# Row transposes at the end of their attention step, their low part one step later, splits and norm-weight products on other steps

## The chip, the cores and the metric

The kernel runs on one core of a Trainium2 chip. The core has five engines: TensorE (PE) for matmuls and transposes, VectorE (DVE), ScalarE (ACT), GpSimd (POOL) and SyncE (SP), which here only starts DMAs. Each takes its own instructions in the order in which they are written, and waits at semaphores that others count up. The metric is the device time of one execution in microseconds, lower is better, as the median of several runs.

## The reference

One decoder block on x of 512 rows (SEQ) and 1024 columns, all in float32:

```python
h = rms_norm(x, g_mix_norm)
z = h @ w_in                      # q, k and v of three branches, gates, zu, zv
# 8 heads of 64, in 2 groups: compressed, selected and window attention
o_attn = g0 * o_cmp + g1 * o_sel + g2 * o_win
o_mix = gelu(zu) * (w_s @ rms_norm(gelu(zv)) + sp_b)
o = concat(rms_norm(o_attn, g_out[:512]), rms_norm(o_mix, g_out[512:]))
x = x + o @ w_out
h = rms_norm(x, g_ffn_norm)
x = x + square(relu(h @ w_ff1)) @ w_ff2
```

With 512 rows the selection takes all eight blocks and the window is as long as the sequence, so the selected and the window branch are both causal attention over the keys seen so far, with their own keys and values.

## The kernel before, in words

Rows are cut into four tiles t of 128. A float32 operand of a large product is kept as two parts, a rounded high part (ACT copies it to fp32r) and a low part (DVE subtracts the high part from the source), and each product is three matmuls, high by high, high by low and low by high (the function three, lines L427 to L429). Weights come by DMA into four raw slots, and are split into high and low part in the same way.

Between the input projection and the feed-forward stage runs the attention loop over 64 steps v, each one (row tile t, head h, branch b): sixteen steps for t = 0, and sixteen for each further tile, with t + 1 key tiles in each. Every engine has its own loop over the steps, written out by hand, in which other work is placed by step number. In step v:

- PE computes the scores of step v + 4 (LEAD = 4, L2018), transposes the weighted probabilities of step v (probs_t, L2057), on odd steps multiplies the probabilities of a pair with the values (values, L2076, LAG = 2), and every fourth step turns a result back (turn_back, L2090).
- ACT copies the transposed probabilities as their high part (pt_high, L1065), and takes the exp of step v + 4 (exp, L1057), which needs DVE's row maximum of it; every fourth step it keeps the values' result (ot_keep).
- DVE takes the row maximum of step v + 4 (row_max, L1505), on even steps the reciprocals of a pair of sums (coefs, L1536), and makes the low part of the transposed probabilities (pt_low, L1528); every eighth step it adds a result to o_sb (combine).
- GpSimd weights the probabilities of a pair (L668, L670) when the reciprocals of the pair are there.

Between these stand the jobs, placed by the table JOBS. Row transposes (rows_t, L1784) turn a tile's rows from o_sb into PSUM as four 128x128 transposes: ("mix", 3, 0) in step 1, ("attn", 0, 0) in 34, ("attn", 1, 0) in 40, ("ffn", 0, 0) in 45, ("ffn", 0, 1) in 50, ("attn", 2, 0) in 55. ACT then makes the high part (ht_hi_evac, L785; for ffn it keeps a raw copy first, raw_keep, L1044; both through job_act), and DVE the low part (ht_lo_evac, L1232). Output projections ("mixo" and "attno", tile, half of the columns) are four chunks c of three matmuls in four steps in a row; chunk 0 is at the end of its step, the others near its start. They follow the row transposes: attno 0 0 in 36 to 39, attno 0 1 in 41 to 44, attno 1 0 in 46 to 49, attno 1 1 in 51 to 54, attno 2 0 in 56 to 59. DVE adds a finished one to xs (add, L1558) at the last of its four steps. All jobs of the loop use one PSUM bank, JB = 3, and each waits until the one before it is taken: a projection until the low part is made, a row transpose until the add is done.

Further work in the loop that the change touches: the split of the feed-forward weights' units 0 and 1 (unit_hi on ACT, L1039; unit_lo on DVE, L1566), 128x1024 each, and ffn_rows (L1226), the product of 512 columns of xs with the norm weight, of which the row transposes of ffn are made: ffn_rows(t, i) must be done before ("ffn", t, i).

After the loop a few more jobs follow in other banks (TAIL). Then comes the feed-forward stage, in units of 24 or 12 matmuls, which is the same before and after.

Of the kernel before, what the change touches and what calls it, by code (L numbers as in the profile page):

```python
# [138 lines left out]
HTN = {k: n for n, k in enumerate(HT)}  # L139
# [78 lines left out]
CHUNKS = {v + c: (k, c) for k, v in JOBS.items() for c in range(steps_of(k))}  # L218
ENDS = {v + steps_of(k) - 1: k for k, v in JOBS.items()}
# [16 lines left out]
def hybrid_block(nc, x, xt, w512, w_c, cmp_w1, cmp_w2, cmp_pe, sp_w, sp_b, g_cols, g_ffn, g_heads, g_sgu,  # L236
                 g_kc, rope, w_ff1, w_ff2, y):
    ctx = ExitStack()
    with ctx:
# [504 lines left out]
        def _(act):  # L744
# [331 lines left out]
            def job_act(k):  # L1076

                if k and k[0] == "ffn":
                    raw_keep(*k[1:])
                if k in HTN:  # L1080
                    ht_hi_evac(*k)
# [6 lines left out]
                exp(v)  # L1088
            for w in range(LEAD, NV + LEAD + LAG):
                s = w - LEAD  # L1090
                job_act(ENDS.get(s))
                if s < NV:
                    pt_high(s)
                if w < NV:
                    exp(w)
                if s >= LAG and (s - LAG) % 4 == 3:
                    ot_keep((s - LAG) // 4)
                if s == 0:
                    ht_hi_evac("mix", 2, 0)
                if s == 2:  # L1100
                    hi(22)
                if s == 10:
                    hi(23)
                if s in (19, 22, 26, 28):
                    hi(24 + (19, 22, 26, 28).index(s))
                if s in (20, 36, 52):
                    act.wait_ge(o_evac, 2 * (s // 16))
                    norm_sum("attn", s // 16 - 1, scr[:, 0:AW])
                if s in (42, 47):
                    unit_hi((s - 42) // 5)  # L1110
                if s in (48, 58):
                    t = (s - 48) // 10
                    act.wait_ge(added, ADD_NO["attno", t, 1] + 1)
                    norm_sum("ffn", t, scr[:, :])
# [71 lines left out]
        def _(dve):  # L1186
# [382 lines left out]
            for w in range(NV + LEAD + LAG + BACK):  # L1569
                s = w - LEAD  # L1570
                k = ENDS.get(s)
                if k in HTN:
                    ht_lo_evac(*k)
                if LEAD <= w < NV:
                    row_max(w)
                if k in ADD_NO:
                    add(*k)
                if 2 <= w <= NV and w % 2 == 0:
                    coefs(w // 2 - 1)
                if 0 <= s < NV:  # L1580
                    pt_low(s)
                if s == 0:
                    ht_lo_evac("mix", 2, 0)
                if s == 3:
                    lo(22)
                if s == 11:
                    lo(23)
                if s in (20, 23, 27, 29):
                    lo(24 + (20, 23, 27, 29).index(s))
                if s in (43, 48):  # L1590
                    unit_lo((s - 43) // 5)
                if s >= LAG + BACK and (s - LAG - BACK) % 8 == 7:
                    combine((s - LAG - BACK) // 16, (s - LAG - BACK) // 8 % 2)
                if s in (41, 45, 52, 56):
                    ffn_rows((s - 41) // 11, {41: 0, 45: 1, 52: 0, 56: 1}[s])


            ffn_rows(2, 0)
# [165 lines left out]
        def _(pe):  # L1764
# [355 lines left out]
            for v in range(NV + LAG):  # L2120
# [5 lines left out]
                product = CHUNKS[v] if v in CHUNKS and CHUNKS[v][0] in ADD_NO else None  # L2126
                if product and product[1] > 0:
                    job(*product)
                if v in CHUNKS and not product:
                    job(*CHUNKS[v])  # L2130
                if v < NV:
                    probs_t(v)
                if v >= LAG:
                    values(v - LAG)
                if product and product[1] == 0:
                    job(*product)
                if v >= LAG + BACK and (v - LAG - BACK) % 4 == 3:
                    turn_back((v - LAG - BACK) // 4)

# [169 lines left out]
```

## Time and profile before

| What | Value |
|---|---|
| median of 3 runs | 591.51 us (590.43 to 591.6) |
| profiled execution | 590.6 us, its span 588.8 us |
| PE busy | 567.9 us, 96% of the span |
| DVE, ACT, POOL busy | 440.7, 359.5, 128.0 us |
| granted TensorE clock | full, in every slice of the span |

The span is what the profile sees of one execution, from the first to the last instruction; the device time lies 1.8 us above it. Busy time of PE is that of its matmuls and transposes, whose modelled ends overlap their successors, so costs are better read from one start to the next. An idle time that the timeline lists stands in brackets behind the instruction that ended it, with what released it.

### The profile page before, as it was taken

The numbers are of one execution on the slowest core, as the hardware profiler recorded it, in microseconds if no ns is written. First come the engines' busy times: TensorE is split into PE (matmuls) and PEld (weight loads), VectorE is DVE, ScalarE is ACT, GpSimd is POOL, SyncE is SP. The second block draws the span as 40 slices with busy tenths as digits, with TensorE's granted clock in tenths as the row PEclk, the third lists the DMA queues.
The fourth block names the chain that finished last, engine by engine and source line by source line (L and its number), as shares of the span: only waits on it lengthen the run. The fifth ranks groups of instructions, "written<-read, shape, count | busy, mean of one in ns | idle before, by whom it ended". The sixth has DMA issues, their size and how long they took to land.

```text
span 588.8 us, 9215 instructions
## 1 busy us (share of the span) xinstructions
PE 567.9 (96%) x3433; PEld 495.8 (84%) x3433; DVE 440.7 (75%) x721; ACT 359.5 (61%) x644; POOL 128.0 (22%) x209
## 2 busy tenths in 40 slices
PE   8999999999889989989999999999999999999997
PEld 7777777887777777868999999999998888888886
DVE  3799890786677878857877675567699996898674
ACT  6866561738676768755673487733697556565551
POOL 1560000002343533510320202211023123020200
PEclk9999999999999999999999999999999999999999
DMA  8933247351112111001997957996879879976862
GB/s 309 336 100 124 93 142 250 107 214 39 53 46 82 37 37 37 1 2 47 188 200 211 176 185 164 187 197 167 208 137 186 216 163 207 243 144 233 175 201 108
DMA packets 25164, 87.56 MB, mean 149 GB/s; under 512 B 3024, under 2 KB 3312, under 8 KB 25120
## 3 DMA queue, kind: packets, MB, share of 16 engines
q0 software_dynamic: 9856, 35.38, 32.1%
q1 hardware_dynamic: 15120, 51.59, 25.3%
q8 instruction: 28, 0.46, 0.3%
q14 instruction: 16, 0.13, 0.1%
q10 hardware_dynamic: 144, 0.00, 0.0%
HBM read 84.87 MB, written 2.10 MB: 148 GB/s over the span
## 4 chain that ended last, share of the span: by engine, by line
PE 80%; DVE 8%; ACT 3%; issue 3%; POOL 3%; DMA 3%; SPq 1%; DVEq 0%; ACTq 0%
PE ps L427 23%; PE ps L429 23%; PE ps L428 23%; PE ps L2057 2%; DMA xT<-in_xt 2%; PE ps L2076 1%; PE ps L1784 1%; PE ps L1927 1%; DMA pe_sb<-in_cmp_pe 1%; DVE ps L1505 1%; DVE w_lo_sb L1203 1%; ACT pt_sb L1065 1%; POOL rope_k L606 1%; PE ps L2018 1%; PE ps L2019 1%
## 5 line engine op out<-in xcount | busy, mean ns | idle before, releaser
L1039 ACT ACTIVATE w_hi_sb<-raw 128x1024 fp32r<-128x1024 f32 x112 | 118.6, 1060 | 114.9 <-PE ps L429 93.3
L1566 DVE TENSOR_TENSOR w_lo_sb<-raw,w_hi_sb 128x1024 fp32r<-128x1024 f32 x112 | 137.1, 1225 | 64.7 <-ACT w_hi_sb L1039 64.4
L680 POOL DMA_DIRECT2D raw<-in_w_ff x64 | 55.5, 867 | 237.5 <-DVE w_lo_sb L1566 213.1
L427 PE MATMUL ps<-w_hi_sb,a_hi 128*128 128x512 f32 x224 | 87.1, 389 | 0.0
L428 PE MATMUL ps<-w_lo_sb,a_hi 128*128 128x512 f32 x224 | 87.1, 389 | 0.0
L429 PE MATMUL ps<-w_hi_sb,a_lo 128*128 128x512 f32 x224 | 87.1, 389 | 0.0
L427 PE MATMUL ps<-w_hi_sb,ht_hi 128*128 128x512 f32 x192 | 78.4, 409 | 4.0 <-DVE ht_lo L1232 1.4
L427 PE MATMUL ps<-ht_hi,w_hi_sb 128*128 128x256 f32 (+1 forms) x272 | 79.1, 291 | 0.0
L429 PE MATMUL ps<-ht_hi,w_lo_sb 128*128 128x256 f32 (+1 forms) x272 | 78.8, 290 | 0.0
L428 PE MATMUL ps<-ht_lo,w_hi_sb 128*128 128x256 f32 (+1 forms) x272 | 78.7, 289 | 0.0
L429 PE MATMUL ps<-w_hi_sb,ht_lo 128*128 128x512 f32 x192 | 75.2, 392 | 0.0
L428 PE MATMUL ps<-w_lo_sb,ht_hi 128*128 128x512 f32 x192 | 75.1, 391 | 0.0
L427 PE MATMUL ps<-S_hi,w_hi_sb 128*128 128x256 f32 x192 | 54.3, 283 | 0.0
L428 PE MATMUL ps<-S_lo,w_hi_sb 128*128 128x256 f32 x192 | 54.3, 283 | 0.0
L429 PE MATMUL ps<-S_hi,w_lo_sb 128*128 128x256 f32 x192 | 54.3, 283 | 0.0
L429 PEld LDWEIGHTS ps<-ht_hi,w_lo_sb 128*128 128x128 f32 x272 | 52.1, 192 | 0.7
L428 PEld LDWEIGHTS ps<-ht_lo,w_hi_sb 128*128 128x128 f32 x272 | 52.2, 192 | 0.6
L427 PEld LDWEIGHTS ps<-ht_hi,w_hi_sb 128*128 128x128 f32 x272 | 52.1, 192 | 0.7
L429 PEld LDWEIGHTS ps<-w_hi_sb,a_lo 128*128 128x128 f32 x224 | 42.0, 188 | 8.8
L427 PEld LDWEIGHTS ps<-w_hi_sb,a_hi 128*128 128x128 f32 x224 | 42.0, 188 | 8.7
L428 PEld LDWEIGHTS ps<-w_lo_sb,a_hi 128*128 128x128 f32 x224 | 42.0, 188 | 8.6
L427 PEld LDWEIGHTS ps<-w_hi_sb,ht_hi 128*128 128x128 f32 x192 | 36.1, 188 | 13.3 <-issue 3.2
(239 smaller groups left out, 1136.3 us busy)
## 6 DMA issues: line engine op xcount, KB each, us to landing
raw<-in_w_ff POOLq DMA_DIRECT2D x64, 512.0 KB, 6.3
raw<-in_w_ff SPq DMA_DIRECT2D x48, 512.0 KB, 4.2
raw<-in_w SPq DMA_DIRECT2D x23, 512.0 KB, 4.4
xs<-in_x SPq DMA_DIRECT2D x8, 512.0 KB, 7.1
raw<-in_cmp_w SPq DMA_DIRECT2D x8, 512.0 KB, 4.3
xT<-in_xt SPq DMA_DIRECT2D x3, 512.0 KB, 9.0
raw<-in_w_c SPq DMA_DIRECT2D x4, 304.0 KB, 3.1
out_y<-xs SPq DMA_DIRECT2D x2, 512.0 KB, 3.2
```

Of the source, the lines that this page charges most:

```text
L427: pe.matmul(out, l_hi, r_hi, start=start, stop=False)
L428: pe.matmul(out, l_hi, r_lo, start=False, stop=False)
L429: return pe.matmul(out, l_lo, r_hi, start=False, stop=stop)
L606: pool.tensor_tensor(out, bc(table, shape), bc(g, shape), ALU.mult).then_inc(rope_made, 1)
L680: pool.dma_start(raw[:, n % RAW, :], (w_ff1, w_ff2)[stage - 1][k, q], accum_op=ALU.add, max_dma_last_dim=8192).then_inc(raw_added[n % RAW] ...
L1039: act.activation(w_hi_sb[:, FS[j], :], raw[:, j, :], ACT.Copy).then_inc(w_hi, 1)
L1065: act.activation(p_parts(v, 0), ps[:, 4 + v % 2, 0:n].rearrange("p (k s) -> p k s", s=P), ACT.Copy).then_inc(pt_hi, 1)
L1203: last = dve.scalar_tensor_tensor(out=l[:, k, :], in0=r[:, k, :], scalar=gcol(n, k), in1=h[:, k, :].bitcast(F32), op0=ALU.mult, op1=ALU.su ...
L1505: dve.tensor_tensor_reduce(out=s, in0=s, in1=causal[:, SEQ - n:], scale=-1.0, scalar=-MASKED, op0=ALU.add, op1=ALU.min, accum_out=nmax[:, ...
L1566: dve.tensor_tensor(w_lo_sb[:, FS[j], :], raw[:, j, :], w_hi_sb[:, FS[j], :].bitcast(F32), ALU.subtract).then_inc(w_lo, 1)
L1784: last = pe.transpose(ps[:, bank, k * P:k * P + P], src[:, k * P:k * P + P], ident[:, :])
L2057: mm = pe.transpose(ps[:, 4 + v % 2, k * P:k * P + P], p_sb[:, v % PB, k * P:k * P + P], ident[:, :])
```

## The change

Four things are moved. On PE the row transposes no longer stand ahead of the step's probability transposes but at its end, behind the values (where chunk 0 of a projection already stands). On ACT the copies of a job (job_act) stand behind pt_high, exp and ot_keep of the step. On DVE the low part (ht_lo_evac) is made one step later, and behind that step's row maximum. The splits of units 0 and 1 are one step earlier on both engines, and the norm-weight products move from steps 41, 45, 52, 56 to 41, 48, 53, 57 (the first argument, the tile, is 0, 0, 1, 1 in both).

```diff
--- before.py
+++ after.py
@@ -1088,13 +1088,13 @@
                 exp(v)
             for w in range(LEAD, NV + LEAD + LAG):
                 s = w - LEAD
-                job_act(ENDS.get(s))
                 if s < NV:
                     pt_high(s)
                 if w < NV:
                     exp(w)
                 if s >= LAG and (s - LAG) % 4 == 3:
                     ot_keep((s - LAG) // 4)
+                job_act(ENDS.get(s))
                 if s == 0:
                     ht_hi_evac("mix", 2, 0)
                 if s == 2:
@@ -1106,8 +1106,8 @@
                 if s in (20, 36, 52):
                     act.wait_ge(o_evac, 2 * (s // 16))
                     norm_sum("attn", s // 16 - 1, scr[:, 0:AW])
-                if s in (42, 47):
-                    unit_hi((s - 42) // 5)
+                if s in (41, 46):
+                    unit_hi((s - 41) // 5)
                 if s in (48, 58):
                     t = (s - 48) // 10
                     act.wait_ge(added, ADD_NO["attno", t, 1] + 1)
@@ -1569,10 +1569,10 @@
             for w in range(NV + LEAD + LAG + BACK):
                 s = w - LEAD
                 k = ENDS.get(s)
-                if k in HTN:
-                    ht_lo_evac(*k)
                 if LEAD <= w < NV:
                     row_max(w)
+                if ENDS.get(s - 1) in HTN:
+                    ht_lo_evac(*ENDS[s - 1])
                 if k in ADD_NO:
                     add(*k)
                 if 2 <= w <= NV and w % 2 == 0:
@@ -1587,12 +1587,12 @@
                     lo(23)
                 if s in (20, 23, 27, 29):
                     lo(24 + (20, 23, 27, 29).index(s))
-                if s in (43, 48):
-                    unit_lo((s - 43) // 5)
+                if s in (42, 47):
+                    unit_lo((s - 42) // 5)
                 if s >= LAG + BACK and (s - LAG - BACK) % 8 == 7:
                     combine((s - LAG - BACK) // 16, (s - LAG - BACK) // 8 % 2)
-                if s in (41, 45, 52, 56):
-                    ffn_rows((s - 41) // 11, {41: 0, 45: 1, 52: 0, 56: 1}[s])
+                if s in (41, 48, 53, 57):
+                    ffn_rows(s // 50, {41: 0, 48: 1, 53: 0, 57: 1}[s])
 
 
             ffn_rows(2, 0)
@@ -2126,14 +2126,12 @@
                 product = CHUNKS[v] if v in CHUNKS and CHUNKS[v][0] in ADD_NO else None
                 if product and product[1] > 0:
                     job(*product)
-                if v in CHUNKS and not product:
-                    job(*CHUNKS[v])
                 if v < NV:
                     probs_t(v)
                 if v >= LAG:
                     values(v - LAG)
-                if product and product[1] == 0:
-                    job(*product)
+                if v in CHUNKS and (not product or product[1] == 0):
+                    job(*CHUNKS[v])
                 if v >= LAG + BACK and (v - LAG - BACK) % 4 == 3:
                     turn_back((v - LAG - BACK) // 4)
```

## Rows read from the trace of the kernel before

**Rows 1.** The page, busy us (share of the span) and instructions of each engine.
```profile
PE 567.9 (96%) x3433; PEld 495.8 (84%) x3433; DVE 440.7 (75%) x721; ACT 359.5 (61%) x644; POOL 128.0 (22%) x209
```

**Rows 2.** Windows: length, busy us of each engine, PE clock, DMA share, GB/s.
```profile
195.00:232.00 37.00, 32.22 (x211) 27.75 (x211) 28.70 (x75) 27.37 (x69) 14.05 (x27) 1.00 0.09 30
...
280.00:580.00 300.00, 300.00 (x1926) 274.76 (x1925) 235.02 (x271) 182.12 (x239) 55.49 (x64) 1.00 0.83 186
```

**Rows 3.** Timeline of PE: start us, us, instructions, idle before them and releaser.
```profile
145.81 0.50 PE L427 MATMUL ps<-w_hi_sb,ht_hi 128*128 128x512 f32 x1 [1.44 <-DVE ht_lo L1232]
...
195.92 0.66 PE L1784 MATMUL ps<-ident,o_sb 128*128 128x128 f32 x4
...
199.60 0.55 PE L2057 MATMUL ps<-ident,p_sb 128*128 128x128 f32 x3 [0.74 <-POOL p_sb L670]
...
206.82 0.60 PE L1784 MATMUL ps<-ident,o_sb 128*128 128x128 f32 x4
207.26 0.49 PE L2057 MATMUL ps<-ident,p_sb 128*128 128x128 f32 x3
207.50 0.42 PE L2018 MATMUL ps<-kT,qT 128*128 128x384 f32 x1
...
208.98 0.40 PE L427 MATMUL ps<-w_hi_sb,ht_hi 128*128 128x512 f32 x1
...
218.01 0.66 PE L1784 MATMUL ps<-ident,o_sb 128*128 128x128 f32 x4 [2.53 <-DVE xs L1558]
218.50 0.49 PE L2057 MATMUL ps<-ident,p_sb 128*128 128x128 f32 x3
...
219.54 0.40 PE L2018 MATMUL ps<-kT,qT 128*128 128x512 f32 x1
...
220.56 0.50 PE L427 MATMUL ps<-w_hi_sb,ht_hi 128*128 128x512 f32 x1
...
229.65 0.65 PE L1784 MATMUL ps<-ident,o_sb 128*128 128x128 f32 x4 [1.33 <-DVE xs L1558]
...
230.50 0.48 PE L2018 MATMUL ps<-kT,qT 128*128 128x512 f32 x1
...
232.44 0.40 PE L427 MATMUL ps<-w_hi_sb,ht_hi 128*128 128x512 f32 x1
...
240.26 0.65 PE L1784 MATMUL ps<-ident,o_sb 128*128 128x128 f32 x4 [0.51 <-DVE xs L1558]
...
242.14 0.38 PE L2090 MATMUL ps<-ident,ot_sb 128*128 128x128 f32 x2
...
243.18 0.48 PE L427 MATMUL ps<-w_hi_sb,ht_hi 128*128 128x512 f32 x1
```

**Rows 4.** Timeline of DVE, steps 34, 40 and 43 to 44.
```profile
197.24 0.69 DVE L1232 TENSOR_TENSOR ht_lo<-ps,ht_hi 128x512 fp32r<-128x512 f32 x1 [0.91 <-ACT ht_hi L785]
...
208.09 0.69 DVE L1232 TENSOR_TENSOR ht_lo<-ps,ht_hi 128x512 fp32r<-128x512 f32 x1 [1.05 <-ACT ht_hi L785]
...
214.21 0.56 DVE L1528 TENSOR_TENSOR pt_sb<-ps,pt_sb 128x384 fp32r<-128x384 f32 x1 [1.06 <-ACT pt_sb L1065]
214.68 1.22 DVE L1566 TENSOR_TENSOR w_lo_sb<-raw,w_hi_sb 128x1024 fp32r<-128x1024 f32 x1
215.81 0.41 DVE L1545 TENSOR_TENSOR o_sb<-o_sb,ps 128x256 f32<-128x256 f32 x1
...
216.60 0.69 DVE L1505 CUSTOM_DVE_ANT_0 ps<-ps,causal 128x512 f32<-128x512 f32 x1
...
217.21 0.75 DVE L1558 SCALAR_TENSOR_TENSOR xs<-ps,rstd,xs 128x512 f32<-128x512 f32 x1
```

**Rows 5.** Timeline of ACT, steps 44 and 45.
```profile
217.38 0.69 ACT L1057 ACTIVATE p_sb<-ps,nmax 128x512 f32<-128x512 f32 x1 [1.85 <-DVE nmax L1505]
...
218.70 0.60 ACT L1044 ACTIVATE ht_raw<-ps 128x512 f32<-128x512 f32 x1 [0.54 <-PE ps L1784]
```

**Rows 6.** Line L1226: count, duration ns min/median/max, first and last start, forms.
```profile
L1226 DVE TENSOR_TENSOR o_sb<-xs,grow_ffn x8: 681/692/1019, 210.9 to 273.4; 128x512 f32<-128x512 f32 x8
```

## Prediction

> **What bounds the kernel.** I read the page's busy shares first: TensorE (PE) is busy 96% of the span, far above the others [rows 1]. Then the windows, since a share over the whole span mixes stages: from 280 to 580 us PE is busy 300.00 of 300.00 us, so the feed-forward stage starts when the attention stage hands over and then runs at its own pace; DVE (235.02) and ACT (182.12) are not full there [rows 2]. The reader is to see that time can only be won or lost ahead of 280 us, and that whatever is won there comes out at the end one for one. Of 195 to 232 us PE is busy only 32.22 of 37.00, so 4.78 us stand open [rows 2]. The timeline of PE then says where: five of its waits hang on the row transposes (L1784). In step 34 they start at 195.92, an estimated 0.27 after PE was through with the scores, which the row does not list as a wait; the probability transposes of step 36 wait 0.74; in step 45 they wait 2.53, in step 50 1.33, in step 55 0.51 [rows 3]. The DVE timeline shows the other face: DVE sits 0.91 and 1.05 us in front of each low part (L1232), because it is first in its step and waits for ACT's high part, and behind it queue the row maximum, the coefficients and the low part of the probabilities [rows 4].
>
> Steps are numbered as in the code. Costs on PE are taken from start to start: row transposes 0.44 (206.82 to 207.26); scores, probabilities and values of a step 1.48 (207.50 to 208.98) and probabilities with values 1.04 (218.50 to 219.54) for three key tiles, so scores 0.44; scores, probabilities and values for four tiles 1.94 (230.50 to 232.44) [rows 3].
>
> **The change, part by part.** No instruction is added or removed: 64 steps with the same matmuls, evictions and loads. Only orders change. So the price is in waits, and I went through each job with its neighbours.
>
> *The new shape of the wait.* Row transposes go into PSUM bank 3, and so does the projection that follows. That projection's chunk 0 stands at the end of its step and must wait for the low part. Before, the rest of the transposes' own step lay in between as well; now only the step after it does. The chain from the transposes' end to the projection is 1.57 us for an attention job (207.26, when the next instruction follows them, to 208.78, the end of the low part at 208.09 + 0.69, and 0.05 to hand over) and 2.06 us for a feed-forward job, which ACT keeps raw first (218.50 to 220.56) [rows 3, 4]. Beside that, the low part now stands behind the row maximum of its step, and ACT's high part behind the exp of its step.
>
> *Step 34 (attn 0).* Probabilities go ahead of the transposes, so the 0.27 is filled. DVE does row maximum 38 and the coefficients of 36 and 37 near 196.8 instead of 1.5 later, behind the low part that began at 197.24 [rows 4], so the weighted probabilities of step 36, which came 0.74 too late, are there before PE asks. So the 0.74 goes too. The projection comes two steps later, with 2.3 us of PE work to cover 1.6 to 2.1. Term: -1.0 us.
>
> *Step 40 (attn 1).* No wait stood here before (206.82) [rows 3]. Now the cover between transposes and projection is the 1.48 us of 207.50 to 208.98; with the high part behind exp 44 (about 0.5 late) the chain is near 2.05, so PE waits 0.55 in step 41. Term: +0.55.
>
> *Weight split 0 (step 43 to 42) and step 45 (ffn 0, half 0).* PE's 2.53 us in step 45 end with the add of DVE (L1558) at 217.21 + 0.75. It was late because one DVE step held low part, weight split 1.13 (214.68 to 215.81) and combine 0.79, and the split itself came after ACT's 1.05 us high half, on which, and then the high part of the probabilities, DVE waited 1.06 [rows 4]. After the change split and combine are in different steps, yet both are still ahead of the add. PE takes up chunk 0 of step 41 at 208.98 - 1.0 + 0.55 = 208.5; with that chunk and the next (0.70 each), scores and probabilities 42 it is at 210.6, and ACT's high part ends at 211.2. From the low part of step 42, near 211.25, DVE has 0.47 + 1.13 (split), then row maximum 0.47 (three quarters of the 0.61 of 216.60), low part 0.47, combine 0.79, then row maximum 48 0.61, add 0.7 [rows 4]: the add ends near 215.9. PE has done probabilities 45 and values 43 by 215.85, so the transposes start at 215.9. But DVE goes on with coefficients and low part 44 (0.54) and row maximum 49 (0.60) to 217.0, ACT then does exp 49 (0.60), the kept values (0.35), the raw copy (0.50) and the high part (0.55) to 219.05 [rows 5], the 0.35 an estimate for half the columns, then DVE the low part (0.69): chunk 0 of the next projection at about 219.8, against 220.56. PE's one wait of 2.53 turns into one of some 2.7 a little later, of which the work pulled ahead hides a part. PE was 0.45 ahead when it came in and is 0.75 ahead when it leaves. Term: -0.3.
>
> *Weight split 1 (48 to 47), norm-weight product 45 to 48, step 50 (ffn 0, half 1).* DVE between low part 47 and the add of step 49, by the same rows: split 1.13, row maximum 0.61, low part 0.6, product 0.69 [rows 6], row maximum 0.61, add 0.7. The split now starts a step sooner. PE comes to its transposes 0.75 sooner than at 229.65 - 1.33 = 228.3, so at 227.6, and the add ends then too: the 1.33 us goes. The price comes one step on: exp 54 and the high part stand in ACT's queue behind the sum of squares of step 48, on 1024 columns like a split's high half, so that exp 54 starts near 228.7; 0.6 for it, 0.5 for the raw copy, 0.5 for the high part and 0.69 for the low part lead to 231.0. PE arrives at 227.6 + 0.44 + 1.94 = 230.0 and waits 1.0. Chunk 0 at 231.0 against 232.44 [rows 3]: 1.44 ahead. Term: -0.7.
>
> *Step 55 (attn 2); products 52 to 53 and 56 to 57.* Before, PE waits 0.51 and some 0.25 more goes in handing over. After, probabilities and values fill the wait for the add, but step 56 has no values: the cover is only 242.14 to 243.18 [rows 3], 1.04 with the gaps and 0.96 without, against row maximum 60 (0.61), which must come after scores 60 (0.8 us in), and then 0.69 of low part: 2.1 at least. PE waits about 1.05. The two products move inside DVE time that is idle by then. Term: +0.25.
>
> *Step 1 (mix 3).* Chunk 0 waits 1.44 us, until 145.81 [rows 3]. Its low part now comes after a row maximum of 256 columns (half of the 0.61, 0.3) but the exp that follows that maximum is about as much sooner. Term: 0, bounds -0.1 and +0.35.
>
> The weight splits free their slots for two feed-forward loads earlier; since PE is full from 280 us, these loads are worth nothing, and nothing else is queued behind them on the sync engine. The row transposes behind the loop stay where they are.
>
> **Sum.** -1.0 + 0.55 - 0.3 - 0.7 + 0.25 + 0 = -1.2 us. The profiled execution took 590.6 us around a span of 588.8; the median of the three runs is 591.51, so 590.6 becomes 589.4, and the median 590.3. The terms are estimates with about 0.3 us each, and one late instruction shifts those after it.
>
> **One rule against one row.** The norm-weight product (two inputs in SBUF) takes 0.69 us in the median and 1.02 at its longest, the one of step 56, which lies beside GpSimd's weighting of probabilities [rows 6]. GpSimd's weighting starts on even steps, and the change moves the products of 52 and 56 to odd steps and a split from 48 to 47, but one product from 45 to 48. If three lengthenings of 0.33 went and one came, that is 0.66 more gain; the operations stand mostly in DVE time that is not on the chain, so the sum takes nothing for it, and it is a rival below. The Trainium skill (SBUF — State Buffer, section Who interferes with whom) says that a DVE instruction with two SBUF inputs and a GpSimd instruction that reads SBUF contend for one shared port, the second one blocked until the first is done; the trace agrees in direction, though by 0.33 us and not by a whole instruction.
>
> **The rivals.**
> *Likeliest (0.50): small gain*, -2.0 to -0.6, about -1.2, as summed: waits are removed at 34, 45, 50 and 55, and a part comes back at the projections.
> *The chain stays inside its cover (0.25).* If exp and row maximum do not get in the way, the exposed parts are only the bare chains less cover: 1.57 - 1.48 = 0.1 at 41, 2.06 - 0.7 = 1.35 at 46 (scores at 219.54 and probabilities), 2.06 - 1.94 = 0.1 at 51, 1.57 - 0.96 = 0.6 at 56, together 2.15, against 0.27 + 0.74 + 2.53 + 1.33 + 0.51 = 5.4 removed [rows 3]: -3.2 us, 588.3. For it speaks that DVE and ACT sit idle about as long as PE in these places; against, that both are in-order queues and the exp stands ahead of the high part.
> *Less hindrance by GpSimd (0.08):* as the likeliest, with 0.7 more: -1.9, 589.6.
> *Slower (0.12).* The place is DVE's queue: the low part behind a row maximum that waits for scores, and PE's chunk 0 behind the low part. It decides from the point where steps 41, 46, 51 and 56 each expose more than the wait before them gave. At step 41 +0.55 and 56 +0.55 have nothing or little to set against; if 46 and 51 come 1.2 later than reckoned (the raw copy and the high part start only after exp 50 and 55, 0.7 and a wait), the sum is -1.0 + 0.55 + 0.9 + 0.5 + 0.55 = +1.5, 593.0.
> *The order does nothing (0.05):* probabilities were the bound all along, and only 34 moves by 0.3; 591.2.
>
> **Numbers.** 0.2% is 1.2 us, about what a measurement of this kernel can tell from no change; my sum lies on that edge. Of the likeliest case half is beyond it, of the second all and of the third nearly so: 0.25 + 0.25 + 0.07 = 0.57 for faster; most of the slower case, 0.10; the rest 0.33. The range runs from just below the second case (588.2) to the milder half of the slower case (592.2); the likeliest case alone covers 589.5 to 590.9.
>
> **What the profile after would show.** Right: row transposes of 34, 45, 50, 55 with no wait for the add; no wait for weighted probabilities in step 36; no idle DVE in front of the low part of step 34; and PE waits in front of chunk 0, for the low part, of about 0.5, 2.7, 1.0 and 1.0 us; 280 us and after as before, shifted. Wrong: if PE's wait in step 46 is under 1.5 us, ACT's order was no hindrance and the gain is nearer 3; if PE waits for probabilities (L2057) more than now, the moved evictions have made DVE late, and it is slower.

## The result, and the profile after

The changed kernel takes 594.66 us in the median of 4 runs (593.15 to 595.4), the kernel before 591.0 beside it (4 runs, 590.43 to 591.6). The ratio is 1.0059, 95% interval 1.0035 to 1.0082: it is slower, by 3.7 us, where 1.2 us less was forecast, and it lies outside the range. The profiled execution of the changed kernel took 593.15 us around a span of 591.4, 2.6 us more than the span before. Two later runs of the kernel before took 701.5 and 1136.2 us, where all its others lie between 590.2 and 593.3; they are counted nowhere below.

The page gives no hint of it. Its row of the granted clock reads 9, the highest step, in each of the 40 slices, as before, and busy shares are those of before, with 2.5 us more of PE [rows 1]:

```profile
PE 570.4 (96%) x3433; PEld 497.8 (84%) x3433; DVE 440.8 (75%) x721; ACT 358.7 (61%) x644; POOL 127.1 (21%) x209
```

The windows say where. From 280 to 580 us nothing changed. In 195 to 232 us PE is busy 33.73 instead of 32.22 us with two instructions fewer, and its granted clock, 1.00 before, is 0.95 [rows 2]. Cut into single microseconds, four of them stand at 0.50 to 0.68:

```profile
195.00:232.00 37.00, 33.73 (x209) 28.82 (x207) 29.40 (x78) 25.95 (x68) 14.62 (x29) 0.95 0.08 29
280.00:580.00 300.00, 300.00 (x1937) 275.18 (x1936) 234.94 (x272) 184.26 (x243) 55.39 (x64) 1.00 0.84 187
...
221.00:222.00 1.00, 1.00 (x4) 0.81 (x3) 0.16 (x1) 0.90 (x1) 0.90 (x3) 0.62 0.00 0
222.00:223.00 1.00, 1.00 (x4) 0.71 (x4) 0.20 (x1) 0.00 (x0) 0.62 (x1) 0.50 0.00 0
223.00:224.00 1.00, 1.00 (x4) 0.70 (x3) 0.56 (x2) 0.00 (x0) 0.00 (x0) 0.50 0.00 0
224.00:225.00 1.00, 1.00 (x8) 1.00 (x7) 0.00 (x0) 0.28 (x1) 0.00 (x0) 0.68 0.00 0
225.00:226.00 1.00, 1.00 (x9) 0.92 (x8) 0.76 (x2) 0.88 (x3) 0.00 (x0) 1.00 0.00 0
```

The timeline of PE in the changed kernel, against [rows 3]: the waits for the add (L1558) have nearly gone, and each projection now waits for the low part.

```profile
146.30 0.50 PE L427 MATMUL ps<-w_hi_sb,ht_hi 128*128 128x512 f32 x1 [1.97 <-DVE ht_lo L1232]
...
199.14 0.47 PE L427 MATMUL ps<-w_hi_sb,ht_hi 128*128 128x512 f32 x1
...
208.88 0.50 PE L427 MATMUL ps<-w_hi_sb,ht_hi 128*128 128x512 f32 x1 [0.53 <-DVE ht_lo L1232]
...
216.72 0.66 PE L1784 MATMUL ps<-ident,o_sb 128*128 128x128 f32 x4 [0.18 <-DVE xs L1558]
...
220.69 0.50 PE L427 MATMUL ps<-w_hi_sb,ht_hi 128*128 128x512 f32 x1 [2.29 <-DVE ht_lo L1232]
...
221.71 0.63 PE L2018 MATMUL ps<-kT,qT 128*128 128x512 f32 x1
222.14 0.63 PE L2019 MATMUL ps<-kT,qT 128*128 128x512 f32 x1
222.56 0.63 PE L427 MATMUL ps<-w_hi_sb,ht_hi 128*128 128x512 f32 x1
...
225.27 0.38 PE L2090 MATMUL ps<-ident,ot_sb 128*128 128x128 f32 x2
225.40 0.48 PE L2018 MATMUL ps<-kT,qT 128*128 128x512 f32 x1
...
230.66 0.66 PE L1784 MATMUL ps<-ident,o_sb 128*128 128x128 f32 x4 [0.20 <-DVE xs L1558]
...
234.43 0.50 PE L427 MATMUL ps<-w_hi_sb,ht_hi 128*128 128x512 f32 x1 [1.26 <-DVE ht_lo L1232]
...
245.84 0.47 PE L427 MATMUL ps<-w_hi_sb,ht_hi 128*128 128x512 f32 x1 [1.05 <-DVE ht_lo L1232]
```

Behind the wait of 2.29 us the matmuls of 512 columns start 0.43 us apart and last 0.63, where at full clock they start 0.23 apart and last 0.40: the lower of the two levels, 1.2 GHz. From the projection's first matmul to the next L2090 PE takes 4.58 us (220.69 to 225.27); the same instructions took 3.01 before (220.56 to 223.57). That is 1.57 us with no wait in it. The rows of the kernel before that this and later sections use, beside [rows 3]:

```profile
199.91 0.47 PE L427 MATMUL ps<-w_hi_sb,ht_hi 128*128 128x512 f32 x1
...
221.83 0.40 PE L427 MATMUL ps<-w_hi_sb,ht_hi 128*128 128x512 f32 x1
...
223.57 0.38 PE L2090 MATMUL ps<-ident,ot_sb 128*128 128x128 f32 x2
```

The chain behind the 2.29 us wait is in the timelines of ACT and DVE in the changed kernel. The transposes end near 217.1; ACT has nothing to do until DVE's row maximum of step 49 (217.10, which waits in DVE's queue behind the add, 215.91, and the low part of step 44, 216.65) lets it start exp 49, and the two copies of the job stand behind that exp:

```profile
217.88 0.69 ACT L1057 ACTIVATE p_sb<-ps,nmax 128x512 f32<-128x512 f32 x1 [0.64 <-DVE nmax L1505]
218.47 0.19 ACT L1057 ACTIVATION_READ_ACCUMULATOR p_sb<-ps,nmax 128x1 f32 x1
218.56 0.37 ACT L1073 ACTIVATE ot_sb<-ps 128x256 f32<-128x256 f32 x1
218.83 0.60 ACT L1044 ACTIVATE ht_raw<-ps 128x512 f32<-128x512 f32 x1
219.30 0.61 ACT L785 ACTIVATE ht_hi<-ps 128x512 fp32r<-128x512 f32 x1
```
```profile
212.26 1.40 DVE L1566 TENSOR_TENSOR w_lo_sb<-raw,w_hi_sb 128x1024 fp32r<-128x1024 f32 x1
...
215.91 0.75 DVE L1558 SCALAR_TENSOR_TENSOR xs<-ps,rstd,xs 128x512 f32<-128x512 f32 x1
...
217.10 0.69 DVE L1505 CUSTOM_DVE_ANT_0 ps<-ps,causal 128x512 f32<-128x512 f32 x1
...
219.94 0.69 DVE L1232 TENSOR_TENSOR ht_lo<-ps,ht_hi 128x512 fp32r<-128x512 f32 x1 [1.02 <-ACT ht_hi L785]
```

The wait list of 136 to 280 us sums it up: 7.1 us for the low part in five waits, 0.4 us for the add in two (before, 1.4 in one and 4.4 in three). For weighted probabilities PE waits less than before, 3.1 against 4.2 us.

```profile
PE ps L427 <- DVE ht_lo L1232: 7.1, 5, 2.3
...
PE ps L2057 <- POOL p_sb L670: 3.1, 5, 1.4
...
PE ps L1784 <- DVE xs L1558: 0.4, 2, 0.2
```

Starts of the same instruction after minus before give the balance: chunk 0 of step 2 +0.49, of which 0.21 is left by 195 us; chunk 0 of step 36 -0.77, of step 41 -0.10, of step 46 +0.13, L2090 behind it +1.70, chunk 0 of step 51 +1.99, of step 56 +2.66, the span +2.6.

### The profile page after: what moved, and what is told of

Same layout as the page of the kernel before. It is cut to its first block, busy times and chain, and to the rows that moved or that the text cites. A ratio compares the mean times of both kernels' runs of the same rounds, so it can differ in the third digit from the quotient of the medians.

```text
span 591.4 us, 9215 instructions
## 1 busy us (share of the span) xinstructions
PE 570.4 (96%) x3433; PEld 497.8 (84%) x3433; DVE 440.8 (75%) x721; ACT 358.7 (61%) x644; POOL 127.1 (21%) x209
## 4 chain that ended last, share of the span: by engine, by line
PE 81%; DVE 8%; POOL 3%; DMA 3%; ACT 2%; issue 2%; SPq 1%; DVEq 0%; ACTq 0%
PE ps L427 23%; PE ps L429 23%; PE ps L428 23%; PE ps L2057 2%; PE ps L2076 1%; DMA xT<-in_xt 1%; PE ps L1927 1%; DMA pe_sb<-in_cmp_pe 1%; PE ps L1784 1%; DVE w_lo_sb L1203 1%; DVE ps L1505 1%; PE ps L2019 1%; PE ps L2018 1%; POOL rope_k L606 1%; DVE pt_sb L1528 1%
## 5 line engine op out<-in xcount | busy, mean ns | idle before, releaser
L427 PE MATMUL ps<-w_hi_sb,ht_hi 128*128 128x512 f32 x192 | 78.9, 411 | 9.4 <-DVE ht_lo L1232 7.1
L427 PE MATMUL ps<-w_hi_sb,a_hi 128*128 128x512 f32 x224 | 87.1, 389 | 0.0
L427 PE MATMUL ps<-ht_hi,w_hi_sb 128*128 128x256 f32 (+1 forms) x272 | 79.1, 291 | 0.0
L427 PE MATMUL ps<-S_hi,w_hi_sb 128*128 128x256 f32 x192 | 54.3, 283 | 0.0
L427 PEld LDWEIGHTS ps<-ht_hi,w_hi_sb 128*128 128x128 f32 x272 | 52.1, 192 | 0.7
L427 PEld LDWEIGHTS ps<-w_hi_sb,ht_hi 128*128 128x128 f32 x192 | 36.2, 189 | 19.3 <-DVE ht_lo L1232 8.4
L427 PEld LDWEIGHTS ps<-w_hi_sb,a_hi 128*128 128x128 f32 x224 | 42.0, 188 | 8.7
```

Of the source, the lines that this page charges most:

```text
L427: pe.matmul(out, l_hi, r_hi, start=start, stop=False)
```

## The experiments

Each run lists its mean granted clock. That of the kernel before takes two values, so its runs have two times: over all its runs beside the twelve experiments 590.5 us in the median at 0.999 or more (35 runs) and 591.7 at 0.997 (49 runs), each with a few runs some 1.3 us higher that the clock doesn't explain. A mean of 0.997 over 590 us is what a few microseconds at half clock make: 4 of 590 at half is 0.997. So ratios below are those of medians over mixed runs, and where the clock decides, the runs are split by it. The first four kernels ran on one chip, the next four on a second, then three on a third, the last by itself, each beside the kernel before.

**1. The changed kernel again.** No edit.

> The changed kernel once more, nothing edited. Theory A (the granted clock): in its profile PE waits 2.29 us in step 46 and then runs at half clock from 220.96 to 224.9 us, which cost 1.6 us there; the runs of 594.6 to 595.4 us have more such stretches than the profiled one of 593.15. So runs of this kernel should spread with their mean clock: near 593 with 0.997, near 595 with 0.994. Theory B (the waits alone: PE stands 0.5, 2.3, 1.3 and 1.05 us in front of chunk 0, the clock is chance): the time should sit near 592 whenever the clock is full.

594.28 us (593.29 to 594.5, 5 runs), 1.0042 [1.0028, 1.0056]; clocks 0.994 and 0.997. The profiled run (593.98) has two stretches at half clock, one as above and one behind the 1.97 us wait of step 2. Windows of it:

```profile
147.00:148.00 1.00, 1.00 (x4) 0.70 (x4) 0.00 (x0) 0.28 (x1) 0.51 (x2) 0.50 0.06 16
148.00:149.00 1.00, 1.00 (x5) 0.73 (x3) 0.00 (x0) 0.16 (x1) 0.00 (x0) 0.50 0.00 0
...
222.00:223.00 1.00, 1.00 (x4) 0.70 (x4) 0.00 (x0) 0.71 (x1) 1.00 (x2) 0.50 0.00 0
223.00:224.00 1.00, 1.00 (x4) 0.81 (x3) 0.36 (x1) 0.00 (x0) 0.42 (x1) 0.50 0.00 0
```

From chunk 0 of step 2 to the L2090 behind it this run takes 7.63 us (146.22 to 153.85), the changed kernel's run without the stretch 6.73 (146.30 to 153.03): 0.90 us more, although a later wait for weighted probabilities (0.45 us at 151.36 in the changed kernel) is gone from it. No run of the changed kernel, of nine, was above 0.997.

**2. The low part back in its own step, on DVE alone.** It stands behind the low part of the probabilities there.

```diff
-                if ENDS.get(s - 1) in HTN:
-                    ht_lo_evac(*ENDS[s - 1])
...
                 if 0 <= s < NV:
                     pt_low(s)
+                if k in HTN:
+                    ht_lo_evac(*k)
```

> The changed kernel, but DVE makes the low part of the row transposes in their own step, at its end, behind the low part of the probabilities, and not behind the next step's row maximum. Theory B: the low part no longer waits for scores of the next step and a row maximum, so 0.4 to 1.0 us of each wait in steps 2, 41 and 56 goes, some 1.5 us together; in steps 46 and 51 ACT's high part is last and little changes; 592 to 593 us. Theory A: if the wait of step 46 stays near 2.3 us the half clock stays with it, and no more than the 1.5 us is won.

594.05 us (592.93 to 594.96, 6 runs), 1.0042 [1.0026, 1.0058]: no change. The waits before chunk 0 are 1.84, 0.54, 2.29, 1.26 and 0.92 us. At steps 41, 46 and 51 DVE's order is not the limit, since DVE has to wait for ACT's high part anyway (0.50 us ahead of the low part in step 41 and 1.68 in step 46 of this run). The profiled run, at 0.994, has half clock behind the 2.29 us wait and also behind the 1.84 us wait of step 2.

**3. Splits and norm-weight products back in their old steps.**

```diff
-                if s in (41, 46):
-                    unit_hi((s - 41) // 5)
+                if s in (42, 47):
+                    unit_hi((s - 42) // 5)
...
-                if s in (42, 47):
-                    unit_lo((s - 42) // 5)
+                if s in (43, 48):
+                    unit_lo((s - 43) // 5)
...
-                if s in (41, 48, 53, 57):
-                    ffn_rows(s // 50, {41: 0, 48: 1, 53: 0, 57: 1}[s])
+                if s in (41, 45, 52, 56):
+                    ffn_rows((s - 41) // 11, {41: 0, 45: 1, 52: 0, 56: 1}[s])
```

> The changed kernel with the weight splits back in steps 42/43 and 47/48 and the norm-weight products back in 41, 45, 52 and 56: the transposes' move alone. Theory B: the split and combine stand together again ahead of the add of step 44, so the add is about 0.7 us later, PE's wait before the transposes of step 45 comes back in part and chunk 0 of step 46 is later by 0.5 to 1 us: 594 to 596 us. Theory A: the total wait around steps 45 and 46 is then longer still, so the half clock comes at least as often. Against both: if this is faster than the changed kernel, it was the splits that hurt.

596.29 us (595.21 to 598.15, 6 runs), 1.0082 [1.0064, 1.01], 2.0 us above run 1. The transposes of steps 45 and 50 wait 0.94 and 0.81 us for the add again, the projections 2.29 and 1.26 as before. The second stretch at half clock is longer here (222.2 to 229.1 us), and a first one stands behind the 1.97 us wait of step 2, so more than the waits came back. Beside the moved transposes, the splits' move is a gain.

**4. The changed kernel with its waits in 46, 51 and 56 filled.** Dummy transposes of the identity go to columns of a PSUM bank that are free then, and nothing reads what they write. The semaphore in front of them tells that DVE has taken that bank's last contents, which it did before, so they begin right behind PE's own work. They take 0.12 us each (2.35 us for 20), so they end about when the low part is there.

```diff
+                if v in (46, 51, 56):
+                    pe.wait_ge(o_evac, 5 if v < 56 else 6)
+                    for _ in range({46: 20, 51: 10, 56: 8}[v]):
+                        pe.transpose(ps[:, 7, 256:256 + P], ident[:, :], ident[:, :])
                 if v in CHUNKS and (not product or product[1] == 0):
                     job(*CHUNKS[v])
```

> The changed kernel, and PE is kept busy in front of chunk 0: 20 dummy transposes of the identity in step 46, 10 in step 51 and 8 in step 56, into half of PSUM bank 7 that is free then; their 0.11 us each lie inside the waits. Theory A: no stretch of half clock, mean clock 1.0 in all runs, and 1.6 to 3 us faster than the changed kernel: 591.5 to 592.5 us, which leaves about 1 us over the kernel before. Theory B: the waits for the low part are unchanged, the time too (594 to 595), or slightly worse.

591.91 us (591.39 to 592.99, 12 runs), 1.001 [0.9999, 1.002]. Seven runs are at a clock of 0.999 or more, 591.39 to 592.07 us, and five at 0.996 or 0.997, 592.33 to 592.99: only the wait of step 2 is left to start a stretch. The profiled run has none. Chunk 0 of step 46 starts at 220.45 behind the dummies, and the matmuls behind them are at full clock:

```profile
217.99 2.35 PE L2136 MATMUL ps<-ident 128*128 128x128 f32 x20
220.45 0.50 PE L427 MATMUL ps<-w_hi_sb,ht_hi 128*128 128x512 f32 x1
220.78 0.40 PE L428 MATMUL ps<-w_lo_sb,ht_hi 128*128 128x512 f32 x1
221.02 0.39 PE L429 MATMUL ps<-w_hi_sb,ht_lo 128*128 128x512 f32 x1
221.25 0.40 PE L2018 MATMUL ps<-kT,qT 128*128 128x512 f32 x1
```

PE does more work, the chain from the transposes to chunk 0 is as long as it was (3.98 us against 3.97), and the kernel is 2.4 us faster: that much of the loss is the clock.

**5. The kernel before with only the splits and products moved** (the reverse of edit 3, on the kernel before).

```diff
-                if s in (42, 47):
-                    unit_hi((s - 42) // 5)
+                if s in (41, 46):
+                    unit_hi((s - 41) // 5)
...
-                if s in (41, 45, 52, 56):
+                if s in (41, 48, 53, 57):
```

> The kernel before, with the weight splits one step earlier and the norm-weight products in 41, 48, 53 and 57, and the row transposes left as they were: the other part of the change alone. Putting these two back in the changed kernel made it 2 us slower, so I expect them to be a gain by themselves: the add of step 44 some 0.7 to 1.3 us earlier, PE's wait of 2.53 us in step 45 down to 1.2 to 1.8, the one of step 50 down by up to 1: 589 to 590.3 us against 591.5. If it is 591 or more, their gain exists only beside the moved transposes.

590.62 us (590.26 to 592.4, 12 runs), 0.9991 [0.9981, 1.0001]. The wait of step 45 falls from 2.53 to 1.92 us, that of step 50 from 1.33 to 1.25, and that of step 55 rises from 0.51 to 1.10 [rows 3]; the ten runs at full clock take 590.47 us in the median, those of before 590.5. What is won at 45 is given back at 55. Beside the moved transposes the same edit is worth 2.0 us (run 3).

**6. ACT's copies of a job ahead of exp, behind pt_high, in the changed kernel.**

```diff
                 if s < NV:
                     pt_high(s)
+                job_act(ENDS.get(s))
                 if w < NV:
                     exp(w)
                 if s >= LAG and (s - LAG) % 4 == 3:
                     ot_keep((s - LAG) // 4)
-                job_act(ENDS.get(s))
```

> The changed kernel, but ACT copies a job (raw and high part) behind the high part of the probabilities and ahead of the exp of its step, and no longer behind exp and kept values. Theory C (ACT's order makes the chain long): in step 45 the copies start as the transposes end, near 217.2, and not at 218.83 behind an exp that waits for DVE's row maximum 49; chunk 0 of step 46 comes about 1.6 us earlier, the wait of 2.29 falls to 0.7, that of step 51 from 1.26 to about 0.2; with it the half clock in step 46 goes: 589 to 591 us. Theory D (the low part's place on DVE makes it long): the waits stay within 0.5 us and the time within 1 us of 594.3.

590.28 us (589.21 to 591.22, 12 runs), 0.9975 [0.9964, 0.9986]: faster than before, and 4.0 us faster than the changed kernel. Five runs at full clock take 589.24 in the median, seven at 0.996 or 0.997 some 1.1 more. The wait of step 46 is halved, as its row in the timeline of PE shows, and no half clock follows it; in the profiled run the one stretch left is at 147 to 151 us, behind the 1.97 us wait of step 2. DVE makes the low part at 219.41 with no idle time before it: the high part is done at 219.1, and what stands ahead in DVE's queue, the row maximum of step 50 (218.80), is now what it waits for.

```profile
220.15 0.50 PE L427 MATMUL ps<-w_hi_sb,ht_hi 128*128 128x512 f32 x1 [1.12 <-DVE ht_lo L1232]
```

**7. Edits 6 and 2 together.**

> Both edits of the two kernels on this: ACT's copies ahead of the exp, and DVE's low part in its own step behind the low part of the probabilities. Theory C: as the one before, and now that the high part is early the low part's place can matter, worth another 0.3 to 1 us in steps 2, 41, 56: 588.5 to 590.5. If DVE then stands in front of the low part and the row maximum behind it is late, it is slower than the high part ahead alone.

587.47 us (587.2 to 588.78, 6 runs), 0.9937 [0.9923, 0.995]: 4.0 us faster than before and 6.8 faster than the changed kernel. All clocks are 1.0. Edit 2, worth nothing alone, is worth 2.8 us beside edit 6 (1.8 against those runs of run 6 that are at full clock): with the copies early, the row maximum ahead of the low part counts. The PE timeline of this version has these waits for the low part, in steps 2, 46, 51 and 56 (none in 41):

```profile
145.82 0.50 PE L427 MATMUL ps<-w_hi_sb,ht_hi 128*128 128x512 f32 x1 [1.64 <-DVE ht_lo L1232]
...
218.10 0.50 PE L427 MATMUL ps<-w_hi_sb,ht_hi 128*128 128x512 f32 x1 [0.88 <-DVE ht_lo L1232]
...
229.19 0.50 PE L427 MATMUL ps<-w_hi_sb,ht_hi 128*128 128x512 f32 x1 [0.16 <-DVE ht_lo L1232]
...
239.93 0.47 PE L427 MATMUL ps<-w_hi_sb,ht_hi 128*128 128x512 f32 x1 [0.39 <-DVE ht_lo L1232]
```

**8. The kernel before with dummy transposes in its waits of steps 2 and 45.** In step 45 they begin when DVE has taken the bank, so 1.26 us of that wait stay idle ahead of them (until 216.36) and 1.31 us are filled.

```diff
+                if v == 45:
+                    pe.wait_ge(o_evac, 5)
+                    for _ in range(10):
+                        pe.transpose(ps[:, 7, 256:256 + P], ident[:, :], ident[:, :])
                 if v in CHUNKS and not product:
                     job(*CHUNKS[v])
...
+                if v == 2:
+                    wait_free(pe, LAST_FILL[3])
+                    for _ in range(12):
+                        pe.transpose(ps[:, 7, 256:256 + P], ident[:, :], ident[:, :])
                 if product and product[1] == 0:
                     job(*product)
```

> The kernel before, with dummy transposes on PE inside its two longest waits of this stretch: 12 in step 2 and 10 in step 45, behind the combine, into the free half of bank 7. Theory A (the clock): the runs of the kernel before lie near 590.5 with a mean clock of 1.0 and near 591.5 to 592.9 with 0.997, so it too loses a stretch in most runs; with PE busy all runs have 1.0 and the median is 590.5 to 591.0. If the median stays at 591.5 with clocks of 0.997, the stretches lie elsewhere.

590.47 us (590.14 to 591.44, 11 runs), 0.9988 [0.9979, 0.9998], all clocks 0.999 or more. The kernel before pays for half clock too, 1.2 us in 49 of its 84 runs.

**9. The kernel before with only PE's order changed** (the last part of the diff).

```diff
-                if v in CHUNKS and not product:
-                    job(*CHUNKS[v])
...
-                if product and product[1] == 0:
-                    job(*product)
+                if v in CHUNKS and (not product or product[1] == 0):
+                    job(*CHUNKS[v])
```

> The kernel before, with only TensorE's part of the change: row transposes at the end of their step; ACT still copies a job first in its step and DVE still makes the low part first in its step, splits and products in their old places. Theory C (what was lost is lost by ACT's and DVE's order): PE's wait for the add is filled with probabilities and values as in the changed kernel, but ACT's queue now stands in front of transposes that come 0.6 to 1.4 us later in the step, with the high part of the probabilities behind it, and DVE's row maximum behind that. I expect 589.5 to 592, no clear gain. If it is 594 or more, moving ACT's and DVE's part was a help and not the loss.

590.9 us (590.41 to 593.35, 11 runs), 1.0 [0.9987, 1.0014]; at full clock 590.63 in the median (7 runs), against 590.5. The transposes of step 45 wait 1.52 us instead of 2.53 and chunk 0 of step 46 waits 0.88, so one wait has become two: no gain, no loss. The moved transposes alone don't make the kernel slow. The other four runs have clocks of 0.994 to 0.997, though no wait of PE in the loop of the profiled run, which is at full clock, is above 1.52 us.

**10. Version 7 with splits and products back in their old steps.**

> The fastest kernel so far (changed kernel, ACT's copies ahead of the exp, DVE's low part at the end of its own step: 587.5) with weight splits and norm-weight products back in their old steps. In the changed kernel that cost 2.0 us, and moved alone in the kernel before they gave nothing with the clock full (590.3 against 590.4). If splits and transposes help each other, this is 588.5 to 589.5; if only the transposes matter, 587.5.

588.68 us (588.56 to 588.99, 5 runs), 0.9957 [0.9941, 0.9973]: 1.2 us above version 7. The waits for the add come back (0.93 and 0.78 us), those for the low part stay (0.88, 0.16, 0.38).

**11. Run 4 with step 2 filled as well** (placed as in run 8), to see whether the wait of step 2 starts the stretch that run 4 has left.

```diff
+                if v == 2:
+                    wait_free(pe, LAST_FILL[3])
+                    for _ in range(16):
+                        pe.transpose(ps[:, 7, 256:256 + P], ident[:, :], ident[:, :])
```

> The changed kernel with dummy transposes in steps 46, 51 and 56 as before, and 16 more in the wait of step 2. With those of 46, 51 and 56 alone, 5 of 12 runs still had a mean clock of 0.996 to 0.997 and took 592.3 to 593.0, the others 591.4 to 592.1. Theory A: that was the stretch at 146 us behind the 1.97 us wait of step 2; now all runs have a clock of 0.999 or 1.0 and the median is 591.4 to 591.8, 1.0 to 1.3 over the kernel before at full clock: the cost of the waits alone. If 0.997 remains in some runs, the stretch at 146 us has another cause.

591.85 us (591.37 to 592.92, 12 runs), 1.0011 [1.0, 1.0023], all clocks 0.999 or more. Seven runs lie at 591.37 to 591.92, five at 592.53 to 592.92; that spread is not the clock's, and the profiled one of the five was later already at step 2 (147.24 against 146.10 in run 4). Its cause stays open. With the clock full throughout, the changed order costs 1.2 to 1.4 us against 590.5, by run 4's seven runs at full clock (591.7 in the median) or by these twelve.

**12. The kernel before with only step 2 filled,** to find which wait its half clock follows.

> The kernel before with the 12 dummy transposes in front of the projection of step 2 alone, and nothing in step 45. About half of the runs of the kernel before are at a mean granted clock of 0.997 and about 1.2 us longer. If their stretch of half clock lies behind the 1.44 us wait of step 2, all runs here are at 0.999 or more and the median is 590.4 to 590.6; if it lies behind the 2.53 us wait of step 45, about half of the runs stay at 0.997 and at 591.4 to 591.8. The output is that of the kernel before.

591.63 us (590.59 to 592.46, 12 runs), 1.0001 [0.9988, 1.0013]; nine runs at 0.997, three at 1.0. So it isn't step 2. The profiled run (591.77) shows the place, in its windows and its timeline of PE:

```profile
218.11 0.66 PE L1784 MATMUL ps<-ident,o_sb 128*128 128x128 f32 x4 [2.54 <-DVE xs L1558]
...
219.82 0.63 PE L2018 MATMUL ps<-kT,qT 128*128 128x512 f32 x1
...
223.16 0.39 PE L427 MATMUL ps<-w_hi_sb,ht_hi 128*128 128x512 f32 x1
```
```profile
219.00:220.00 1.00, 1.00 (x8) 1.00 (x8) 0.08 (x1) 1.00 (x3) 0.83 (x2) 0.70 0.00 0
220.00:221.00 1.00, 1.00 (x5) 0.70 (x4) 1.00 (x2) 0.27 (x1) 0.00 (x0) 0.50 0.00 0
221.00:222.00 1.00, 1.00 (x5) 0.90 (x4) 1.00 (x4) 0.70 (x3) 0.00 (x0) 0.50 0.00 0
```

The wait of step 45 is 2.54 us here and 2.53 in the profiled run of before [rows 3], and here half clock follows it. From those transposes to the second chunk's L427 PE takes 5.05 us (218.11 to 223.16), before 3.82 (218.01 to 221.83): 1.23 us, near the 1.2 between the two times of the kernel before. The same wait with the same instructions behind it thus has the drop in some executions and not in others.

## Why the prediction was wrong

Two steps failed. The first: the prediction wrote "So the price is in waits", beside a table that has the clock full in every slice, and its sum had no term for what a long wait of PE does to the work behind it. That is the largest single term of the profiled run, 1.57 us. The second: the terms of the waits came to +1.09 us where -1.2 was forecast. Their mechanism was right and their sizes were not, above all in steps 50/51 and 45/46. So the clock is not the whole miss: at full clock on both sides the change is still slower, 591.7 us (run 4) against 590.5. By the prediction's own terms, measured from start to start in the two profiled runs:

| Term | Predicted | Measured |
|---|---|---|
| step 1/2 | 0 | +0.21 (+0.49 at step 2) |
| step 34 to 36 | -1.0 | -0.98 |
| step 40/41 | +0.55 | +0.67 |
| split 0, step 45/46 | -0.3 | +0.23 |
| half clock, steps 46 to 48 | none | +1.57 |
| split 1, step 50/51 | -0.7 | +0.29 |
| step 55/56 | +0.25 | +0.67 |
| sum | -1.2 | +2.66 |

*The order of events was right.* The four waits foreseen in front of the projections, 0.5, 2.7, 1.0 and 1.0 us, are 0.53, 2.29, 1.26 and 1.05. The waits for the add and the 0.74 us of step 36 went, the row transposes of step 34 start without one, 280 us and after are unchanged. Two signs were wrong: DVE still stands 0.23 us in front of the low part of step 34, where none was foreseen, and PE waits less for weighted probabilities than before (3.1 against 4.2 us), though the kernel is slower. The rival in which the chain stays inside its cover is refuted by the 2.29, as its own bound of 1.5 us said. The slower rival named DVE's queue, the low part behind a row maximum, and ACT's copies behind an exp only in brackets; run 2 takes the first away and gains nothing. What binds first is ACT's queue: run 6 moves only its two copies and gives 4.0 us back, 2.4 of them with the clock full on both sides (591.7 in run 4, 589.2 in run 6). DVE's queue binds next, as run 7 shows. Of the rival in which GpSimd hinders less, one part came: the norm-weight product of step 56 no longer takes 1.02 us. But only that one had been lengthened, the one of step 52 took 0.69 before, and now the one of step 48 takes 0.81 and stands ahead of the add for which step 50 waits.

*The clock (shown).* Runs 4 and 11 leave the late chain in place and only keep PE at work in the wait: 2.4 us come back, and no half clock stands behind step 46. In the kernel before, runs 8 and 12 differ only in the ten dummies of step 45: with them 11 of 11 runs are at 0.999 or more, without them 3 of 12. Run 1 shows a drop behind the 1.97 us wait of step 2 too, at 0.90 us. What is left at full clock on both sides, 591.7 (run 4, seven runs) against 590.5, is the price of the waits themselves, 1.2 us, near the 1.1 that the table gives without its clock term. A hint was there to be read: the kernel before had a wait of 2.53 us, and its three runs lay at 590.43 to 591.6 us, two groups; I took 591.51 against the profiled 590.6 for plain spread. The drop follows the 2.29 us in all four profiled runs that have it (the changed kernel, runs 1, 2 and 3), a wait of 2.53 or 2.54 us in step 45 in one of two, and a wait of 1.97 us in step 2 in three of five (runs 1, 3 and 6, not the changed kernel's and not run 4's). It follows one of 1.84 us (run 2) and not one of 1.92 (step 45 of run 5). So the length alone doesn't decide; what else does stays open.

*Split 0, step 45/46 (off by 0.53).* Two sizes. The split was reckoned at 1.13 us from start to start and took 1.32 (212.26 to 213.58); its own duration is 1.40, before 1.22 beside an idle GpSimd [rows 4]. It now begins while GpSimd still weights probabilities (two instructions of 1.31 us together from 211.28), which fits with the longer duration; no run tests it alone. Most of the rest is in the low part of the probabilities in front of it, at 211.78 where I had 211.25, of which 0.35 is what PE had already lost at steps 2 and 41. The chain from the transposes to chunk 0 was right: 3.97 us against 3.9.

The second split shows the other side: it leaves its overlap with GpSimd (1.44 us before, 1.22 after). The Trainium skill (SBUF — State Buffer, section Who interferes with whom) has the loser of the shared port fully blocked; the rows agree that the two disturb each other, by 0.2 us here. They don't tell whether one is blocked fully, since GpSimd had only 0.33 us left when the first split began.

*Split 1, step 50/51 (off by 0.99).* The largest miss among the waits, in two parts. The first, 0.61 us, lies ahead of the transposes. From the L2090 at 225.27 to them PE gained 0.69 us on the kernel before (+1.70 to +1.01), where the sum had 1.30 (-0.75 to -2.05): the probabilities of step 50 now stand ahead of them (229.86, 0.36 us), which the sum left out, and of the wait for the add 0.20 us is left. The second, 0.37 us, is the chain behind them, 3.77 us against 3.4. I timed exp 54 by ACT's queue alone, from 228.7 behind the sum of squares. It waits for DVE's row maximum, which stands behind the add on which PE's transposes wait too, as I had it at step 45 and left out here. The timeline of ACT shows it, 1.24 us behind the transposes (230.66):

```profile
231.90 0.69 ACT L1057 ACTIVATE p_sb<-ps,nmax 128x512 f32<-128x512 f32 x1 [0.33 <-DVE nmax L1505]
```

So this chain too keeps its length, 3.77 us from transposes to chunk 0 (3.78 in run 3, 3.77 in run 4), and moves with PE; being early at step 50 could not win what I booked.

*Step 55/56 (off by 0.42).* The new wait was right (1.05). The 0.25 us "in handing over" that should have gone did not go: 1.05 against the 0.51 of before is +0.54, and 0.13 is left unassigned. *Steps 40/41 and 1/2* were off by 0.12 and 0.21; at step 2 the low part behind the row maximum costs 0.53 us (1.97 against 1.44), above the bound of 0.35, of which a shorter wait at 151 us (0.45 instead of 0.74) gives a part back.

*Between 593.15 and 594.66.* The profiled run is the fastest of the changed kernel's four and has one stretch at half clock; run 1's has two. That, and the spread of 1.3 us seen at one and the same clock, is all that I can say of the rest.

## What to carry to other kernels

When an edit moves a wait to another place of TensorE's queue, price not only its length but the matmuls behind it at half clock, as a term that may come in some executions and not in others (in the profiled runs it came behind waits from 1.84 us up), and list the runs by their granted clock before reading a difference of 0.2%. A copy on which the critical engine waits belongs ahead of any instruction of its own queue that waits for a third engine; follow each queue to that engine's queue, at every place where the pattern recurs. Edits on two engines of one chain are tested together: the low part's move gave nothing alone and 2.8 us once ACT's copies were early.

## What the runs showed of the hardware

Behind waits of TensorE of 1.84 to 2.54 us in the loop the granted clock fell to 0.50 (1.2 GHz) for some 3 us, in run 3 once for 6.8, in some profiled runs and not in others. The fall began between 0.6 us before the end of the wait (run 3) and 1.3 us behind it (run 12). One fall cost 0.90 us (run 1, step 2), 1.23 (run 12) and 1.57 (the changed kernel). No profiled run shows it behind a wait of 1.64 us or less, but that is no safe bound: four of run 9's eleven runs have a mean clock of 0.994 to 0.997, and its profiled run has no longer wait in the loop than 1.52 us. Where those four fall isn't known. Dummy transposes of 0.12 us each in the waits prevented it (run 11: 12 of 12 runs at 0.999 or more).

The Trainium skill (TensorE: Matmul & The Clock Gate, section Why this matters for your kernels) names idle gaps between bursts of matmuls as what brings the lower clock back; the windows of the changed kernel agree in kind, 1.00 ahead of the wait and 0.50 behind it.
